# Sample selection of a sparse attention: quarters sorted by a network of maxima and minima in place of 33 rounds of MAX8

## The reference, cut to what matters

```
ki_all = jnp.concatenate([ki_past, ki], axis=1)
isc = indexer_scores(qi, ki_all, wi)                      # (8, 4, 1028)
adm = jnp.arange(L)[None, :] <= (past + jnp.arange(S))[:, None]
isc = jnp.where(adm[None], isc, -jnp.inf)
vals, sel = lax.top_k(isc, topk)                          # topk = 256
...
return sparse_attend(q, kg, vg, jnp.isfinite(vals))
```

## Time and profile before

| | us |
|---|---|
| runs of the kernel, three | 1467.61, 1470.28, 1473.64 |
| their median | 1470.28 |
| the profiled execution, its span | 1474.8 |
| TensorE busy in it | 1406.1 (95%) |
| VectorE busy | 1088.5 (74%) |
| ScalarE busy | 329.9 (22%) |
| GpSimd busy | 359.9 (24%) |

### The profile page before, as it was taken

One profiled execution on the slowest core, in us unless ns is written; L12 is line 12 of the kernel. 1 busy time (PEld: TensorE's weight loads), 2 busy tenths in 40 slices (PEclk: granted clock), 3 DMA queues, 4 the chain that ended last, 5 costly groups with the idle time before them and its releaser, 6 DMA issues.

```text
span 1474.8 us, 28290 instructions
## 1 busy us (share of the span) xinstructions
PE 1406.1 (95%) x11458; PEld 1291.0 (88%) x11458; DVE 1088.5 (74%) x1392; ACT 329.9 (22%) x653; POOL 359.9 (24%) x304
## 2 busy tenths in 40 slices
PE   6999999999878998999999999999999999999997
PEld 6999999995433886999999999999996669999997
DVE  7977686767976647788768597769578677787764
ACT  3111102003244432321110221110202452211110
POOL 2533212000630021443321253321200003533210
PEclk9999999999997999999999999999999879999998
DMA  8443542664876203554436344345161305344142
GB/s 310 150 171 114 185 166 91 222 211 157 279 287 249 71 4 118 197 197 170 143 124 227 132 163 159 140 145 206 72 225 59 149 33 221 143 171 165 54 160 89
DMA packets 62699, 233.14 MB, mean 158 GB/s; under 512 B 9003, under 2 KB 18545, under 8 KB 45581
## 3 DMA queue, kind: packets, MB, share of 16 engines
q1 hardware_dynamic: 50426, 224.56, 42.7%
q10 hardware_dynamic: 11554, 6.37, 1.5%
q0 software_dynamic: 624, 0.87, 0.2%
HBM read 225.54 MB, written 6.10 MB: 157 GB/s over the span
## 4 chain that ended last, share of the span: by engine, by line
PE 51%; DVE 5%; ACT 1%; DMA 1%; POOL 1%; issue 1%; DVEq 0%; POOLq 0%; SPq 0%
PE psum L191 15%; PE psum L193 15%; PE psum L192 15%; DVE pair_hi L177 1%; DMA ring<-in_w_gu 1%; DVE ring_r L186 1%; DVE x L393 1%; PE psum L235 1%; PE psum L236 1%; DVE hidden_hi L389 1%; PE psum L240 1%; DVE rstd L297 1%; POOL hidden L305 0%; POOL hidden L307 0%; PE psum L351 0%
## 5 line engine op out<-in xcount | busy, mean ns | idle before, releaser
L191 PE MATMUL psum<-x_hi_r,pair_hi 128*128 128x288 f32 x1736 | 516.3, 297 | 6.0 <-DVE up L598 2.7
L193 PE MATMUL psum<-x_hi_r,ring_r 128*128 128x288 f32 x1736 | 515.0, 297 | 0.0
L192 PE MATMUL psum<-x_lo_r,pair_hi 128*128 128x288 f32 x1608 | 474.8, 295 | 0.0
L186 DVE TENSOR_TENSOR ring_r<-ring,pair_hi 128x2048 fp32r<-128x2048 f32 (+1 forms) x127 | 340.2, 2679 | 4.3
L191 PEld LDWEIGHTS psum<-x_hi_r,pair_hi 128*128 128x128 f32 x1736 | 328.8, 189 | 8.6 <-issue 8.1
L193 PEld LDWEIGHTS psum<-x_hi_r,ring_r 128*128 128x128 f32 x1736 | 328.2, 189 | 0.0
L192 PEld LDWEIGHTS psum<-x_lo_r,pair_hi 128*128 128x128 f32 x1608 | 303.4, 189 | 0.3
L191 PE MATMUL psum<-hidden_hi_r,down_hi 128*128 128x288 f32 x704 | 208.4, 296 | 0.0
L192 PE MATMUL psum<-hidden_r,down_hi 128*128 128x288 f32 x704 | 207.7, 295 | 0.0
L193 PE MATMUL psum<-hidden_hi_r,down_r 128*128 128x288 f32 x704 | 207.0, 294 | 0.0
L177 DVE CAST pair_hi<-ring 128x2048 fp32r<-128x2048 f32 (+1 forms) x126 | 161.7, 1283 | 11.8 <-DMA ring<-in_w_gu 10.4
(11 more groups left out here) (547 smaller groups left out, 1856.8 us busy)
## 6 DMA issues: line engine op xcount, KB each, us to landing
ring<-in_w_gu SPq DMA_DIRECT2D x88, 1024.0 KB, 4.8
down<-in_w_down SPq DMA_DIRECT2D x64, 704.0 KB, 4.3
ring<-in_w_ab SPq DMA_DIRECT2D x18, 1024.0 KB, 5.2
ring<-in_w_cd SPq DMA_DIRECT2D x12, 1024.0 KB, 6.2
ring<-in_cache_k SPq DMA_DIRECT2D x32, 256.0 KB, 4.6
index_keys<-in_cache_k SPq DMA_DIRECT2D x32, 256.0 KB, 5.1
index_keys<-in_cache_i ACTq DMA_DIRECT2D x64, 64.0 KB, 2.7
eight_pages_ds<-in_cache_v SPq DMA_DIRECT2D x16, 256.0 KB, 4.8
```

The lines of the kernel that those rows point to most:

```text
L186: return eng.tensor_tensor(lo, a, hi.bitcast(F32), ALU.subtract)
L191: pe.matmul(out, w_hi, x_hi, start=start, stop=False)
L192: pe.matmul(out, w_hi, x_lo, start=False, stop=False)
L193: return pe.matmul(out, w_lo, x_hi, start=False, stop=stop)
```

## The change

Each quarter of 256 past scores is now sorted by a bitonic network: `LEVELS` holds 36 levels, each of which is a maximum and a minimum over 128 pairs (72 instructions). The first level of each run length m (8 of them) reverses the order of the right half; to spare that, right halves are held negated, and a SCALAR_TENSOR_TENSOR with factor -1 does the comparison (the first level of a run, L2051), while the others are TENSOR_TENSOR (L2053). The signs at the start come from a new constant input `signs`, 128 by 256, which GpSimd's queue loads. The 8 columns of new keys are left out of the sort and join at the end: `threshold` reduces the 256 remaining maxima to the 16 smallest, sorts these with MAX8, and compares them with the row's new keys. `STEPS` takes the place of `ROUNDS`: 11 levels ahead of head 0, 18 ahead of head 1, 25 ahead of head 2, all 36 and the join of the quarters ahead of head 3, four of the eight merge levels behind each of heads 3 and 4. `threshold` now stands behind head 5 (before: ahead of head 7), `select` behind head 6 (before: behind head 7), and the eight merge levels behind heads 3 and 4 (before: behind head 5).

```diff
@@ -1466,7 +1466,9 @@
 PAST = 1024
 NPG = 8
 QW = KS + 8
-ROUNDS = (6, 10, 14, 26, 28, 31, 33, 33, 33)
+LEVELS = tuple((m, m >> e) for m in (1 << i for i in range(8)) for e in range(m.bit_length()))
+SORTED = len(LEVELS)
+STEPS = (11, 18, 25, SORTED + 1, SORTED + 5, SORTED + 9, SORTED + 9, SORTED + 9, SORTED + 9)
 KEYS = PAST + NS
 CHUNKS = ((0, 512), (512, 512), (PAST, NS))
 SCALE_A = 64 ** -0.5
...
@@ -1537,8 +1539,10 @@
         mp = z[:, 8:10, 0:TP]
         above = ymix[0:NS, 4:8].rearrange("p a t -> p (a t)")[:, 0:KEYS]
         quarters = z[:, 10:16].rearrange("p a t -> p (a t)")
-        iq, wq, sq = (quarters[:, i * QW:(i + 1) * QW] for i in range(3))
-        moved, pa_, pb_ = (quarters[:, 3 * QW + i * KS:3 * QW + (i + 1) * KS] for i in range(3))
+        iq = quarters[:, 0:QW]
+        wq, sq, moved, pa_, pb_ = (quarters[:, QW + i * KS:QW + (i + 1) * KS] for i in range(5))
+        signs = moved
+        least, newest = (quarters[0:NS, QW + 5 * KS + 16 * i:QW + 5 * KS + 16 * i + 16] for i in range(2))
         n_above, n_equal, kth = (sb(n, [NS, 1]) for n in ("n_above", "n_equal", "kth"))
         xflat = c.xscratch[:, :].rearrange("p k t -> p (k t)")
         pa = xflat[:, 0:4 * TP].rearrange("p (a b t) -> p a b t", a=2, b=2)
...
@@ -1633,6 +1637,9 @@
         def gpsimd(pool):
             pool.wait_ge(z_done, 1)
             pool.memset(qi[:, :, :, :, :], 0.0).then_inc(S["qz_zero"], 1)
+            pool.wait_ge(S["qi_done"], 1)
+            pool.wait_ge(S["ip_sum"], 16)
+            pool.dma_start(signs, c.ins["signs"]).then_inc(S["q_moved"], 16)
             pool.wait_ge(c.pair_done, first + npairs + 2)
             pool.wait_ge(S["qz_zero"], 1)
             pool.memset(qz[:, :, :, :], 0.0).then_inc(S["qz_zero"], 1)
...
@@ -2026,47 +2033,69 @@
 
             dve.wait_ge(S["is_used"], 12)
             dve.wait_ge(S["mp_done"], 1)
+            dve.wait_ge(S["q_moved"], 16)
             dve.tensor_copy(iq[:, 0:KS], B[5][:, 0:KS]).then_inc(S["is_out"], 1)
             dve.tensor_tensor(iq[:, KS:QW], B[5][:, KS:QW], nmask[:, 0:8], ALU.add).then_inc(S["is_out"], 1)
-            dve.wait_ge(S["is_out"], 2)
-            ln(dve.tensor_scalar(wq, iq, nmask[:, 8:9], None, ALU.mult))
-
-            def top_eight(i):
-
+            dve.wait_ge(S["is_out"], 1)
+            ln(dve.tensor_tensor(wq, iq[:, 0:KS], signs, ALU.mult))
+
+            def level(i):
+
+                m, d = LEVELS[i]
+                a, b = (wq, sq) if i % 2 == 0 else (sq, wq)
+                av, bv = (x.rearrange("p (n e d) -> p n e d", e=2, d=d) for x in (a, b))
                 if i:
-                    dve.wait_ge(S["ts_rep"], i)
-                dve.max(sq[:, 8 * i:8 * i + 8], wq).then_inc(S["ts_max"], 1)
-                if i < QW // 8 - 1:
-                    dve.wait_ge(S["ts_max"], i + 1)
-                    dve.match_replace(out=wq, in_to_replace=sq[:, 8 * i:8 * i + 8], in_values=wq, imm_value=TAKEN).then_inc(S["ts_rep"], 1)
-
-            def merge_quarters():
-
-                dve.wait_ge(S["ts_max"], QW // 8)
-                dve.tensor_copy(moved[quarter(0)], sq[quarter(1), 8:QW])
-                ln(dve.tensor_copy(moved[quarter(2)], sq[quarter(3), 8:QW]))
-                dve.scalar_tensor_tensor(pa_[quarter(0)], moved[quarter(0)], -1.0, sq[quarter(0), 0:KS], ALU.mult, ALU.max)
-                ln(dve.scalar_tensor_tensor(pa_[quarter(2)], sq[quarter(2), 0:KS], -1.0, moved[quarter(2)], ALU.mult, ALU.min))
-                a, b = pa_, pb_
-                d = KS // 2
-                while d >= 1:
-                    av, bv = (x.rearrange("p (m e d) -> p m e d", e=2, d=d) for x in (a, b))
-                    dve.tensor_tensor(bv[0:96, :, 0], av[0:96, :, 0], av[0:96, :, 1], ALU.max)
-                    last = dve.tensor_tensor(bv[0:96, :, 1], av[0:96, :, 0], av[0:96, :, 1], ALU.min)
-                    if d == 1:
-                        last.then_inc(S["ts_max"], 1)
+                    dve.wait_ge(S["ts_max"], i)
+                for e, op in enumerate((ALU.max, ALU.min)):
+                    if d == m:
+                        last = dve.scalar_tensor_tensor(bv[:, :, e], av[:, :, 1], -1.0, av[:, :, 0], ALU.mult, op)
                     else:
-                        ln(last)
-                    a, b = b, a
-                    d //= 2
+                        last = dve.tensor_tensor(bv[:, :, e], av[:, :, 0], av[:, :, 1], op)
+                last.then_inc(S["ts_max"], 1)
+
+            def join_quarters():
+
+                dve.wait_ge(S["ts_max"], SORTED)
+                dve.tensor_copy(moved[quarter(0)], wq[quarter(1)])
+                ln(dve.tensor_copy(moved[quarter(2)], wq[quarter(3)]))
+                dve.scalar_tensor_tensor(pa_[quarter(0)], moved[quarter(0)], -1.0, wq[quarter(0)], ALU.mult, ALU.max)
+                dve.scalar_tensor_tensor(pa_[quarter(2)], wq[quarter(2)], -1.0, moved[quarter(2)], ALU.mult, ALU.min).then_inc(S["ts_max"], 1)
+
+            def merge_level(i):
+
+                d = KS >> (i + 1)
+                a, b = (pa_, pb_) if i % 2 == 0 else (pb_, pa_)
+                av, bv = (x.rearrange("p (n e d) -> p n e d", e=2, d=d) for x in (a, b))
+                dve.wait_ge(S["ts_max"], SORTED + 1 + i)
+                dve.tensor_tensor(bv[0:96, :, 0], av[0:96, :, 0], av[0:96, :, 1], ALU.max)
+                dve.tensor_tensor(bv[0:96, :, 1], av[0:96, :, 0], av[0:96, :, 1], ALU.min).then_inc(S["ts_max"], 1)
+
+            def sorting(i0, i1):
+
+                for i in range(i0, i1):
+                    if i < SORTED:
+                        level(i)
+                    elif i == SORTED:
+                        join_quarters()
+                    else:
+                        merge_level(i - SORTED - 1)
 
             def threshold():
 
-                dve.wait_ge(S["ts_max"], QW // 8 + 1)
+                dve.wait_ge(S["ts_max"], SORTED + 9)
                 ln(dve.tensor_copy(moved[quarter(0)], pa_[quarter(2)]))
-                dve.wait_ge(S["q_moved"], 128)
-                ln(dve.scalar_tensor_tensor(pb_[quarter(0)], moved[quarter(0)], -1.0, pa_[quarter(0)], ALU.mult, ALU.max))
-                ln(dve.tensor_reduce(kth[:, :], pb_[quarter(0)], AX_X, ALU.min))
+                ln(dve.scalar_tensor_tensor(pb_[quarter(0)], pa_[quarter(0)], -1.0, moved[quarter(0)], ALU.mult, ALU.min))
+                ln(dve.tensor_tensor(pa_[quarter(0), 0:128], pb_[quarter(0), 0:128], pb_[quarter(0), 128:256], ALU.max))
+                ln(dve.tensor_tensor(pb_[quarter(0), 0:64], pa_[quarter(0), 0:64], pa_[quarter(0), 64:128], ALU.max))
+                ln(dve.tensor_tensor(pa_[quarter(0), 0:32], pb_[quarter(0), 0:32], pb_[quarter(0), 32:64], ALU.max))
+                ln(dve.tensor_tensor(pb_[quarter(0), 0:16], pa_[quarter(0), 0:16], pa_[quarter(0), 16:32], ALU.max))
+                dve.wait_ge(S["q_moved"], 144)
+                dve.max(newest[:, 0:8], iss[:, PAST:KEYS])
+                ln(dve.max(least[:, 0:8], pb_[quarter(0), 0:16]))
+                ln(dve.match_replace(out=pb_[quarter(0), 0:16], in_to_replace=least[:, 0:8], in_values=pb_[quarter(0), 0:16], imm_value=TAKEN))
+                ln(dve.max(least[:, 8:16], pb_[quarter(0), 0:16]))
+                ln(dve.scalar_tensor_tensor(least, least, -1.0, newest, ALU.mult, ALU.max))
+                ln(dve.tensor_reduce(kth[:, :], least, AX_X, ALU.min))
                 ln(dve.tensor_scalar(above, iss[:, :], kth[:, 0:1], None, ALU.is_gt))
                 dve.tensor_reduce(n_above[:, :], above, AX_X, ALU.add)
                 ln(dve.tensor_scalar(iss[:, :], iss[:, :], kth[:, 0:1], None, ALU.is_equal))
...
@@ -2080,24 +2109,23 @@
                 ln(dve.tensor_scalar(iss[:, :], rank[:, :], -NEG, NEG, ALU.mult, ALU.add))
                 dve.tensor_tensor(iss[:, PAST:KEYS], iss[:, PAST:KEYS], nmask32[:, :], ALU.add).then_inc(S["ms_done"], 1)
 
-            for i in range(ROUNDS[0]):
-                top_eight(i)
+            sorting(0, STEPS[0])
             sample_queries()
+            dve.memset(newest[:, 8:16], TAKEN)
             for h in range(8):
-                if h == 7:
-                    threshold()
                 head(h)
-                for i in range(ROUNDS[h], ROUNDS[h + 1]):
-                    top_eight(i)
-                    if i == ROUNDS[h] + 1:
-                        norm(h)
-                if ROUNDS[h] == ROUNDS[h + 1]:
+                if STEPS[h] == STEPS[h + 1]:
                     norm(h)
+                else:
+                    sorting(STEPS[h], STEPS[h] + 2)
+                    norm(h)
+                    sorting(STEPS[h] + 2, STEPS[h + 1])
                 if h >= 3 and h % 2:
                     out((h - 3) // 2)
                 if h == 5:
-                    merge_quarters()
-            select()
+                    threshold()
+                if h == 6:
+                    select()
             out(3)
             def masked(g):
                 for ch, (c0, w) in enumerate(CHUNKS):
...
```

(8 more changed lines are left out.)

## The result

The changed kernel takes 1485.53 us (median of 20 runs, 1476.12 to 1494.65), the kernel before 1471.74 (20 runs, 1467.61 to 1484.72). The ratio on record is 1.0071, interval 1.0051 to 1.0091: slower, with the lower end just above 0.5%. The profiled execution has a span of 1484.2 us against 1474.8.

What follows compares the result with a forecast made beforehand. TensorE was taken to bound the kernel, the edit paying only where it waits for VectorE; port contention delays head 3 by 17 us and mask products by 12.3, so 1470.3 + 12.3 gives 1482.6 us, range 1470 to 1488.

Steps and rivals of the forecast that it cites:

- One such VectorE instruction passes per GpSimd instruction: Between heads 2 and 3: 27 VectorE instructions alternate with GpSimd's mixing, head 3 at 422.5, 17 us late; full alternation given 0.62.
- each member waited for a GpSimd instruction of its own: Earlier trace's join: both copies and both comparisons, though independent pairs, were read as each waiting for a separate GpSimd instruction.
- partial rival: Levels beside the mixing: maximum and minimum pass together, head 3 near 410.5, mask products near 446, 1473.8 us; chance 0.17.
- The clock: TensorE: lower clock assumed when it resumes at head 3, transposes 1.1 us; plus or minus 2 us in the range.
- From the last transposes to the last product of the recurrence 4.9: TensorE behind head 7's scaling: 4.9 us needed, taken from the earlier trace, putting mask products at about 455.
- the wait for head 7: TensorE ahead of its last transposes: waits for head 7's scaling, expected at 450.5.
- Behind the mask products nothing changes: Rest of the program: the 12.3 us delay at the mask products carries through to the end uncovered.
- a free level 0.52: VectorE away from the mixing: 0.52 us per sorting level, 18.7 us for all 36, 13.8 less than the rounds.
- GpSimd's chain 30 to 31 us: GpSimd's 27 mixing instructions: 30 to 31 us in place of 28.7, about 0.06 more per instruction slipping in.
- threshold 5.7: VectorE behind head 5: the threshold grows from 3.9 to 5.7 us.
- selection 6.0: VectorE between heads 6 and 7: the selection takes 6.0 us, as in the earlier trace.
- no wait for the transfer at the second key products: TensorE behind head 7's products: cache pages have long landed, second key products start near 438.5 without waiting.

Runs made afterwards that it cites:

- e1: The changed kernel with GpSimd's 27 mixing instructions cut to one of 14 columns: 1476.02 us, ratio 1.0028 to the kernel before.
- e2: The kernel before with GpSimd's 27 mixing instructions cut to one of 14 columns: 1476.93 us, ratio 1.0021 to the uncut kernel before.
- e3: The changed kernel with each TENSOR_TENSOR sorting level's minimum waiting for its maximum's semaphore: 1493.25 us, ratio 1.0156 to the kernel before.
- e5: The changed kernel with GpSimd's mixing held back until the join of the quarters is done: 1477.26 us, ratio 1.0008 to the kernel before.
- e6: The changed kernel with GpSimd's mixing held until the join is done and the selection back behind head 7: 1474.33 us, ratio 1.0010 to the kernel before.
- e7: The changed kernel with six extra unused TensorE products ahead of the last transposes: 1485.14 us, ratio 1.0077 to the kernel before.
- e8: The changed kernel with GpSimd's mixing behind the last merge level and the selection behind head 7: 1480.10 us, ratio 1.0019 to the kernel before.
- e4: The changed kernel with the selection moved back behind head 7: 1479.31 us, ratio 1.0042 to the kernel before.

## Why the prediction was right, and where its terms were off

The predicted 1482.6 is 2.9 below the measured 1485.53; the range holds it, and slower was the likeliest sign. The cause given, that VectorE's two-input instructions wait for those of GpSimd's mixing, is shown by e1 and e2 (no mixing, no difference), e3 (doubling the contention) and e5 and e6 (mixing later, slowdown gone). How many of them wait was wrong, and so was the clock, and the two errors cancelled in part. The Trainium skill's rule ("SBUF — State Buffer", section "SBUF: two separate sides"), an exclusive lock held for the whole instruction, agrees with the level of 1.30 against 0.52 us. A single-input copy of 256 elements waited too (1.00 against 0.28). The terms:

- **"One such VectorE instruction passes per GpSimd instruction"** failed for the very instructions that it was used on. It holds for the join (1.00 to 1.35 each), the threshold (e6) and linked pairs (e3). A level's pair passes together, 1.30 us a level. Head 3 is 8.9 us late, not 17. In the rows, a minimum starts 0.08 us ahead of the end of its maximum (402.71 against 402.79), a copy 0.01 behind the end of the one before it (410.55 against 410.54). That this overlap is what lets a second one through is my reading; e3 shows only that linking the two takes it away. Closeness alone isn't enough, as the merge pair at 415.05 shows; in the rows named here, the one that starts no later than GpSimd's next instruction passes (402.71, and 423.27 in e6), and the one that starts behind it waits (415.25, 410.55). The prediction named this as the partial rival, gave it 0.17, and argued against it from the copies and comparisons in the earlier trace rows, as if these stood for a level. It also misread them: "each member waited for a GpSimd instruction of its own" doesn't hold for the first copy, which took its free 0.28 us in the kernel before:

```profile
416.36 0.28 DVE L2046 COPY z<-z 32x256 f32<-32x256 f32 x1
```


- **The partial rival's own price** was low too: head 3 at 410.5 for 414.25. It had the join nearly free, which took 4.7 us (409.54 to 414.25), and GpSimd began at 390.18 and no longer 391.41, so that two levels ahead of head 2 were hit and head 2 came at 394.14, not 392.5. The mechanism that held had been given mask products at 446 and a time of 1473.8, which is 11.7 us too low.
- **The clock.** "From the last transposes to the last product of the recurrence 4.9" was 7.8, since TensorE had stood still 3.34 us ahead of them (e7: 4.9 without the standstill). The prediction had the wait for head 7 and took the clock for it from the earlier trace rows, where the wait was 0.47. It applied the lower level to head 3 and not here. A wait alone doesn't decide it: in e5 the transposes ran at the higher level behind 2.51 us.
- The first of these errors made the forecast too late, the clock made it too early. Mask products: predicted 455, measured 450.97 and 451.43. The forecast of the time owes part of its closeness to that.
- **"Behind the mask products nothing changes"** stands, as far as can be told: the two profiled pairs give 8.2 and 6.9 us late at the masks, 7.6 on average, and 1.0071 is 10.4 us (7.5 to 13.4 by its interval; the medians differ by 13.8). The interval's lower end and the 7.6 meet; whether 2 or 3 us are lost behind the masks stays open, since single executions vary by more.
- **Right:** a free level 0.52; GpSimd's chain 30 to 31 us (30.7), though its reason, 0.06 us for each single instruction that slips in, fails in e3, where they slipped in singly and the chain stayed at 28.6; threshold 5.7 (5.6); selection 6.0 (5.9); no wait for the transfer at the second key products, though at 430.83 and not 438.5.

**Where the 13.8 us saved on VectorE went.** The 11 levels ahead of head 3 would have taken 5.7 us; beside the mixing they took 14.4 (395.06 to 409.50, a reciprocal among them), more than the 12 rounds before. But free of the port there is nothing gained either: VectorE then waits 2.35 to 3.43 us for TensorE at head 3 (e1, e5, e6, e8), and TensorE 3.1 to 7.8 us for the cache pages, whose products start at 424.8 to 428.0 in these as in the kernel before. From this I conclude that a saving on VectorE could count only if the pages came earlier; that wasn't tried. Running part of the mixing earlier, beside rounds of MAX8 in a mixed scheme, wasn't tried.

## What to carry to other kernels

Before replacing one kind of VectorE instruction by another, look at what GpSimd does in that stretch: MAX8 and MATCH_REPLACE8 pass it, while two-input instructions and even small copies wait for the GpSimd instruction that runs. If the two can't be parted in time, leave out waits between independent instructions, so that two can pass together. Check how the long VectorE instructions stand to GpSimd's too: there it is GpSimd that waits (e8). And profile the unchanged kernel twice: a difference behind the point where the edit ends may be one that the old kernel has too.

## What the runs showed of the hardware

- Whether VectorE's instructions pass GpSimd's one or two at a time depends on how they are queued: 1.30 us for an independent maximum and minimum, 2.2 to 2.35 for a linked pair (e3). An instruction that started together with GpSimd's next one took its free time, one that started 0.06 us behind it waited 1.26 us. It was one behaviour in the prediction.
- The wait doesn't depend on the size: a halving of 32x32 took 1.19 us beside the mixing (e6) and 0.18 in the changed kernel, where the mixing was over. Even a two-column TENSOR_SCALAR took 1.07 us at 419.83 in the changed kernel, against 0.17.
- GpSimd hardly pays beside short VectorE instructions, 2.0 us on 28.7 in the changed kernel and nothing in e3, but beside a scan of 2.42 us one of its instructions took 3.06 us in place of 1.13 (e8).
- The granted clock of identical code differs from one execution to the next (0.98 and 0.90 over the same 100 us), and after an 11.84 us standstill the lower level lasted until about 421.5 in one execution and 427.9 in another (e4).
